# A two-block transformer kernel on one core: where two weight splits, the last score copies and the steps of the heads' closing norm stand at the end of the first linear recurrence

## The reference

```python
h = x @ a_w_in[layer]
q, f_raw, i_in, g, qm = jnp.split(h, [768, 1536, 2304, 3072], axis=-1)
seq_out = hgrn2_mix(q, f_raw, i_in, g, lb_all[layer], a_gnorm[layer])
# hgrn2_mix: gated linear recurrence over 6 heads of 128 features,
#   S_t = diag(f_t) S_{t-1} + k_t^T v_t ;  o_t = q_t S_t, and then
o = o * lax.rsqrt(jnp.mean(jnp.square(o), axis=-1, keepdims=True) + RMS_EPS)
o = o * gnorm.reshape(6, 128)
o = o.reshape(B, S, 768) * jax.nn.silu(g)
mixed = jnp.concatenate([seq_out, mem_out], axis=-1)
x = post_norm(x, mixed @ w_o[layer], ...)
x = post_norm(x, hier_moe(x, ...), ...)      # 4 groups x 4 experts
```

## Time and profile before

| what | value |
|---|---|
| median of 3 runs | 1426.18 us (1424.24 to 1428.61) |
| the profiled execution | 1429.56 us, span of its instructions 1427.9 us |
| PE busy | 1352.4 us, 95% of the span |
| DVE busy | 1036.7 us, 73% |
| ACT busy | 774.1 us, 54% |
| granted TensorE clock, mean | 0.973 of full speed |
| DMA | 327.72 MB, 230 GB/s over the span |

### The profile page before, as it was taken

One profiled execution on the slowest core, in us unless ns is written; L12 is line 12 of the kernel. 1 busy time (PEld: TensorE's weight loads), 2 busy tenths in 40 slices (PEclk: granted clock), 3 DMA queues, 4 the chain that ended last, 5 costly groups with the idle time before them and its releaser, 6 DMA issues.

```text
span 1427.9 us, 19509 instructions
## 1 busy us (share of the span) xinstructions
PE 1352.4 (95%) x7484; PEld 1162.3 (81%) x7484; DVE 1036.7 (73%) x1078; ACT 774.1 (54%) x787; POOL 85.2 (6%) x81
## 2 busy tenths in 40 slices
PE   4989999999999899999999899999998989999995
PEld 4977878888899788887999788888878978888884
DVE  7768778887677674545566757888886466789886
ACT  2766543334444534443482546777764565677773
POOL 0000001010000000000000014000004000400000
PEclk9999999999899999999999998999999999999998
DMA  9967578997575575554542433999994522599990
GB/s 358 388 251 235 178 254 305 299 311 272 203 269 177 173 267 179 178 192 160 181 138 98 145 105 122 339 345 347 349 324 122 162 73 90 176 334 348 349 352 31
DMA packets 208909, 327.72 MB, mean 230 GB/s; under 512 B 9456, under 2 KB 146352, under 8 KB 208832
## 3 DMA queue, kind: packets, MB, share of 16 engines
q1 hardware_dynamic: 195536, 276.71, 57.2%
q0 software_dynamic: 13296, 49.93, 10.3%
HBM read 325.56 MB, written 1.05 MB: 229 GB/s over the span
## 4 chain that ended last, share of the span: by engine, by line
PE 81%; DVE 11%; ACT 3%; DMA 3%; SPq 1%; issue 1%; DVEq 0%; ACTq 0%; POOLq 0%
PE ps L2250 23%; PE ps L2252 23%; PE ps L2251 23%; DVE w_low L1431 2%; DMA scratch<-in_w_ada 2%; ACT w_high L701 1%; DMA raw<-in_w_qkv 1%; PE ps L2788 1%; PE ps L3000 1%; PE ps L2630 1%; DVE stats L1968 1%; PE ps L2361 1%; DVE h_low L2124 1%; DVE scratch L1479 1%; DVE x_rows L1959 1%
## 5 line engine op out<-in xcount | busy, mean ns | idle before, releaser
L1431 DVE TENSOR_TENSOR w_low<-raw,w_high 128x2048 fp32r<-128x2048 f32 x254 | 583.4, 2302 | 249.1 <-ACT w_high L701 247.1
L701 ACT ACTIVATE w_high<-raw 128x2048 fp32r<-128x2048 f32 x254 | 484.2, 1908 | 305.7 <-PE ps L2252 279.2
L2250 PE MATMUL ps<-w_high,h_high 128*128 128x512 f32 (+1 forms) x888 | 352.4, 397 | 9.6 <-DVE h_low L1556 4.7
L2252 PE MATMUL ps<-w_high,h_low 128*128 128x512 f32 (+1 forms) x888 | 345.2, 389 | 0.0
L2251 PE MATMUL ps<-w_low,h_high 128*128 128x512 f32 (+1 forms) x888 | 345.2, 389 | 0.0
L2250 PEld LDWEIGHTS ps<-w_high,h_high 128*128 128x128 f32 x888 | 168.2, 189 | 44.9 <-issue 8.9
L2252 PEld LDWEIGHTS ps<-w_high,h_low 128*128 128x128 f32 x888 | 168.4, 190 | 34.9
L2251 PEld LDWEIGHTS ps<-w_low,h_high 128*128 128x128 f32 x888 | 168.6, 190 | 32.0 <-issue 0.2
L2250 PE MATMUL ps<-h_high,w_high 128*128 128x256 f32 x592 | 173.4, 293 | 6.2 <-DVE h_low L1556 6.1
L2251 PE MATMUL ps<-h_low,w_high 128*128 128x256 f32 x592 | 169.3, 286 | 0.0
L2252 PE MATMUL ps<-h_high,w_low 128*128 128x256 f32 x592 | 169.1, 286 | 0.0
(11 more groups left out here) (377 smaller groups left out, 1492.5 us busy)
## 6 DMA issues: line engine op xcount, KB each, us to landing
raw<-in_w_down SPq DMA_DIRECT2D x124, 512.0 KB, 4.9
raw<-in_w_gate_up SPq DMA_DIRECT2D x88, 512.0 KB, 5.3
scratch<-in_w_ada POOLq DMA_DIRECT2D x40, 1024.0 KB, 5.5
raw<-in_w_gate SPq DMA_DIRECT2D x80, 512.0 KB, 5.0
raw<-in_w_up SPq DMA_DIRECT2D x80, 512.0 KB, 6.2
raw<-in_w_qkv SPq DMA_DIRECT2D x24, 512.0 KB, 13.9
raw<-in_w_o SPq DMA_DIRECT2D x24, 512.0 KB, 4.7
raw<-in_w_in SPq DMA_DIRECT2D x24, 512.0 KB, 5.2
```

Source lines behind the costliest of these rows:

```text
L701: act.activation(wh[u % SPL][:, :, 0:w], raw[u % RAW][:, :, 0:w], ACT.Copy).then_inc(h_split, 1)
L1431: dve.tensor_tensor(wl[u % SPL][:, :, 0:w], raw[u % RAW][:, :, 0:w], wh[u % SPL][:, :, 0:w].bitcast(F32), ALU.subtract).then_inc(l_split, 1)
L2250: pe.matmul(o, h1, h2, start=start, stop=False, skip_group_check=True)
L2252: return pe.matmul(o, l1, h2, start=False, stop=stop, skip_group_check=True)
```

## The change

It moves instructions and waits within the engines' orders; nothing is computed otherwise. On DVE the split of wo1+1 goes from behind level (7, 0) to behind the last level, and the split of wo1+2 from ahead of the gain-and-gate loop to behind `outs_low(2)`; the order of the pairs is now scaled, low, scaled, low. On ACT the two copies of level 8 go ahead of and right behind the gate's copy, the split of wo1+2 goes behind `outs_high(2)`, and roots and high parts are reordered. On PE the wait for the gate's copy goes from ahead of all heads to ahead of the first sum of squares, and the filling matmuls (`keep_busy`) are split in two, 3 and 4.

```diff
@@ ACT @@
                 late_take(7, u)
+            late_take(8, 0)
             done(6)
             features(16, 2, ACT.Silu)
             lin[0] += 1
+            late_take(8, 1)
             act.activation(hh[:, HG:HG + 2, :], FT[:, 18:20, :], ACT.Copy).then_inc(hh_ready, 1)
             hhr.up()
-            for u in range(2):
-                late_take(8, u)
             act.preload_act_table_set("natural_log_exp_and_others")
-            ahead(PLAN["wo1"])
@@ ACT @@
             root_logs(0)
+            roots(0)
             squares(2)
-            roots(0)
             root_logs(1)
+            outs_high(0)
             roots(1)
-            outs_high(0)
             root_logs(2)
+            outs_high(1)
             roots(2)
-            outs_high(1)
             outs_high(2)
+            ahead(PLAN["wo1"])
             router_high(208)
             ahead(PLAN["wo1"] + 3)
@@ DVE @@
-            SPLITS_IN = {(3, 0): 10, (4, 0): 11, (5, 1): 12, (7, 0): 13}
+            SPLITS_IN = {(3, 0): 10, (4, 0): 11, (5, 1): 12}
             for l in range(8):
...
+            ahead(PLAN["a_in"] + 13)
             dve.wait_ge(hh_ready, hhr.up())
             dve.tensor_tensor(hl[:, HG:HG + 2, :], FT[:, 18:20, :], hh[:, HG:HG + 2, :].bitcast(F32), ALU.subtract).then_inc(ol_ready, 1)
             dve.wait_ge(ol_ready, olr.up())
             dve.wait_ge(lin_evac, 21)
-            ahead(PLAN["wo1"])
             for a in range(3):
@@ DVE @@
             outs_scaled(0)
+            outs_low(0)
             outs_scaled(1)
-            outs_low(0)
+            outs_low(1)
             outs_scaled(2)
-            outs_low(1)
             outs_low(2)
+            ahead(PLAN["wo1"])
@@ PE @@
             olr.up()
-            pe.wait_ge(lin_evac, lin[0])
             exr.n = 3
...
                 if h == 3:
+                    pe.wait_ge(lin_evac, lin[0])
                     head_squares(0)
             head_squares(1)
+            keep_busy(3, 3)
+            head_squares(2)
             keep_busy(4, 3)
-            head_squares(2)
             out_rows(fresh=True)
```

## The result

The changed kernel is slower: median 1431.05 us (1426.94 to 1432.99, 20 runs) against 1425.29 us of the kernel before (1423.25 to 1429.16, 20 runs). The ratio of the times is 1.0031, with a 95% interval of 1.0021 to 1.0042, so 3 to 6 us were lost, where 3 were expected to be won. The second timing gave 1.0021 (1.0009 to 1.0033). The profiled execution took 1427.13 us, span 1425.4 us, and this is 2.4 us *less* than the profiled execution of before. So all positions here are counted from that first product, which I call the mark.

What follows compares the result with a forecast made beforehand. PE's own stream was taken to bound the kernel (81% of the chain). A gain of 3.75 us, limited by the row-load chain, less 0.7 for colliding loads gave 3.05: median 1426.18 to 1423.1 us, range 1419.6 to 1426.8.

Steps and rivals of the forecast that it cites:

- (e): POOL's row loads through the wo1+3 split bind PE's fourth projection unit: about 1.5 us pause, leaving 3.75 us gain.
- (f): SP's 1 MB expert load, released by the moved wo1+2 split, meets POOL's nine DMAs: 0.7 us, bounds nothing to 3.0.
- a drain: On ACT ahead of `squares(0)`, a drain of about 1380 ns with the table load would leave 1.7 us gain.
- The rule of turns: DMA engines alternate packets between queues, so POOL's last constant tiles (448 KB, 1.3 us) take twice as long.
- rival C: Closing norm starts later, through clock at 0.50 or a pause behind the table load: gain 1.65, time 1424.5 us; chance 0.12.
- B: SP's load beside POOL's list costs 1.3 to 3.0 us, by turns or more; time 1423.7 to 1425.4 us; chance 0.20.
- D: POOL's row loads beside SP's load land at least 3.75 us late, eating the shift: slower, 1427.1 us; chance 0.05.

Runs made afterwards that it cites:

- the loads held: Changed kernel, with SP waiting for POOL's nine row loads before its expert-stage loads from the third unit on; 1425.59 us, ratio 0.9991 to the kernel before.
- the pause filled: Changed kernel plus 20 fill matmuls on PE ahead of the projection's fourth unit; ratio 1.0009 to the kernel before.
- the third split alone: Kernel before with only the wo1+2 split moved, behind the last high part on ACT and last low part on DVE; 1431.28 us, ratio 1.0027.
- the pairs alone: Kernel before with only the closing norm reordered to scaled, low, scaled, low, with matching ACT order and fill matmuls in two parts; ratio 1.0018.
- the levels alone: Kernel before with only the wo1+1 split behind DVE's last level, level 8 copies around the gate's, and PE's gate wait moved; ratio 1.0000.

## Why the prediction was wrong

**The positions up to the last low part were right.** Predicted behind the mark: products of (8, 1) at 1.3, the gain-and-gate loop's end at 9.8, the projection at 12.1, the last low part at 16.5. Measured: 1.34, 9.86, 12.25, 16.60. Also right was that another chain ends later, (e), the one over POOL's rows, ACT's wait and the split of wo1+3. With the loads held, so that (f) is out of it, its sum is met within 0.5 us (33.7 and 34.14). ACT's next instruction started 0.02 us behind the table load (803.85 + 1.28 to 805.15), so nothing came of a drain.

**The step that failed is (f), the price of the collision.** I took 0.7 us and a bound of 3.0. It measured 3.3 and 3.6 us: 12.8 and 13.1 us from POOL's first issue to ACT against 9.5 before. The row that I took it from, a load of 512 KB that meets SP's loads with nothing behind it in a list, was the wrong neighbour: here the last three of nine loads each landed about 3 us later (7.4, 7.3 and 7.8 us against 4.7, 4.4 and 4.5). The bound was near the truth: it was the load's whole time at full rate, and the load took 3.2 us of all DMA engines and delayed the last tile by about as much. What was wrong was to expect a quarter of it.

The rule of turns named in (f) (the Trainium skill, DMA: Bandwidth & Descriptors, Queues, rings and completion order) gives the right sign. The delay of 1.3 us that the prediction worked out from it is an estimate, which takes the turns to be equal in bytes; it is less than half of what these runs show.

**What was left out is the clock behind the new pause.** Step (e) gave PE a pause of 1.5 us at the fourth unit (1.34 with the loads held), the collision made it 4.57, and the clock was low for 6.8 us from its last part on. The prediction priced low clock only at the place where the trace of before had it (rival C), not at the place where it made a new pause. The run with the pause filled puts 2.1 to 2.6 us on it.

**And the baseline was read from one execution.** The stage was 37.43 us in the profile that the sum went by, and 35.85 and 35.81 in two others. The prediction said itself that the profiled execution was 3.4 us above the median, but treated this as an offset that stays, while 1.6 us of it were in the very pauses that the change was to remove, as low clock. A gain in such a pause is smaller by that in a usual execution. Together, in the middle: -3.05 + 1.6 (baseline) + 2.75 (collision, 3.45 less 0.7) + 2.35 (clock) = +3.65 us for the stage, which stands 3.5 and 4.0 us above the usual one of before, and in the times 4.4 and 3.0 us above (ratios times 1426).

**The rivals.** By the prediction's own sign (POOL's loads over 10.8 us) B is what happened, and the delay of 3.3 and 3.6 us lies just above its 1.3 to 3.0. By B's reckoning a small gain would be left, 0.45 to 0.15 us. The outcome, slower, is D's, and so is the place, but D's condition, a delay from 3.75 us on, was not met. What stands between B's delay and D's outcome are the two things that no rival had in it: the low clock behind the new pause (2.1 to 2.6 us) and the baseline (1.6 us). The order of the pairs was costed as free at the first pair and 1.8 us at the last, and both sizes are right; but it was counted as part of a gain, and alone it loses: 1.6 us of the stage, 2.6 us by the ratio.

**What stays open.** Why the last tiles waited for the whole load, and did not share the time with it, was not taken apart further (sizes and kinds of the single pieces were not varied). A meeting of both queues doesn't always cost this: in the kernel before, the second layer's list of six loads runs beside two loads of SP (issued at 1084.75 and 1085.17, the list from 1087.20 on), and its 512 KB rows landed in 3.9 and 5.1 us, where they took 4.2 and 5.1 alone. Also open is why the same pause is followed by low clock in one execution and not in the next.

## What to carry to other kernels

When a split, copy or other step that frees a buffer is moved, the load which it releases moves too: look what other transfers are under way at the new time, and who waits for them in order. A wait for many small loads should not stand ahead of work that the bounding engine needs, since the time to spare there is eaten by anything that delays the loads; here one more split put ahead of the wait turned 0.3% lost into no change (0.9994), and with the old order of the pairs it became 0.25% won. A pause that is removed is worth what it costs in several executions, not in one: take two or three traces of the kernel before when the difference sought is of the size of one stretch of low clock, and count from a mark just ahead of the change.

## What the runs showed of the hardware

- Two DMAs of 512 KB from SP beside a list of nine from POOL took 8.2 us each to landing, and the last three of the list 7.3 to 7.8 us instead of 4.4 to 4.7. SP's took 3.8 us each at its old place in the kernel before. The last of the list came later by 3.3 and 3.6 us, and the load's share of all DMA engines was 3.2 us.
- A full DMA share doesn't mean a high rate: in the kernel before, 8 GB/s at a share of 1.00 (829.00 to 830.00) while nothing but the end of POOL's list was under way, against 345 GB/s at 1.01 in the earlier trace rows.
- The same pause can be followed by a stretch at 0.50 or not: PE's 2.19 us ahead of the projection was followed by one in the first trace of before and not in the two others. The pause of 2.45 us was followed by one in all three of these traces and in that of the third split alone, and by none with the pairs alone. The new one of 4.57 us had 6.8 us at 0.50, and the norm's first row came 5.1 us behind the unit's start (834.54 to 839.66) instead of 2.9.
- A shorter pause was not always a gain: with the levels alone a pause of 2.45 us became one of 0.4 and one of 2.42 us later, with the low clock behind the second, and the time did not change.
